# An encoder kernel on one core: in the first layer, the powers of the input matrices are each worked out from the raw matrices, held in PSUM

## The reference, cut to what matters

```
a_bar = exp(lam * dt)                                  # complex, one per state
b_bar = ((a_bar - 1.0) / lam)[..., None] * b_mat       # b_mat = b_re + i b_im
bu    = einsum('gph,bsgh->bsgp', b_bar, u)
states[s] = a_bar * states[s-1] + bu[s]                # in both directions
```

## Time and profile before

| | |
|---|---|
| median of 3 runs | 1513.65 us (1512.05 to 1514.21) |
| the profiled execution | 1514.12 us, of which the traced span is 1512.3 us |
| busy over the span | PE 94%, PEld 77%, DVE 76%, ACT 59%, POOL 22% |
| GpSimd's products (lines 394 to 400) | all in the two mixers |
| mean DMA rate | 248 GB/s |
| mean granted clock of TensorE | 0.979 of full speed |

### The profile page before, as it was taken

How to read it: one execution, slowest core, us unless ns; L and a number is a source line. 1 busy time by engine, 2 the same in 40 slices (tenths; PEclk the granted TensorE clock), 3 DMA queues, 4 the chain that set the end, 5 groups by cost and what they waited for, 6 DMA issues and landing times.

```text
span 1512.3 us, 24141 instructions
## 1 busy us (share of the span) xinstructions
PE 1421.9 (94%) x8701; PEld 1163.8 (77%) x8701; DVE 1145.3 (76%) x1098; ACT 897.7 (59%) x988; POOL 336.2 (22%) x427
## 2 busy tenths in 40 slices
PE   4689999999998999898999999999999999999995
PEld 3567778788887788677888888878888888788884
DVE  6965656755546477576889889988898889888985
ACT  4335454543435365645767776767677767776774
POOL 3895740999100077100000000000000000000000
PEclk9899899999999999998999999999999999999998
DMA  9242144555554433594999999999999999999970
GB/s 262 94 170 72 57 139 168 180 184 183 190 166 167 144 95 113 172 336 141 366 353 338 364 333 347 361 320 362 343 338 362 330 351 365 314 363 331 349 255 28
DMA packets 273809, 374.65 MB, mean 248 GB/s; under 512 B 17616, under 2 KB 220752, under 8 KB 273616
## 3 DMA queue, kind: packets, MB, share of 16 engines
q1 hardware_dynamic: 270176, 367.51, 71.7%
q0 software_dynamic: 1280, 3.15, 1.1%
q10 hardware_dynamic: 2288, 3.11, 0.6%
HBM read 371.63 MB, written 1.05 MB: 246 GB/s over the span
## 4 chain that ended last, share of the span: by engine, by line
PE 79%; DVE 9%; ACT 5%; issue 4%; DMA 1%; SPq 1%; POOL 0%; ACTq 0%; DVEq 0%; POOLq 0%
PE bank L579 76%; ACT hi L1050 3%; DVE lo L1411 3%; SPq L454 1%; PE bank L980 1%; PE bank L597 1%; DVE raw L394 1%; DVE at_lo L1836 1%; DVE raw L396 1%; DMA areg<-in_norm_mix_dram 1%; DMA raw<-in_w_out_dram 1%; DVE at_lo L1806 1%; DVE at_lo L1425 0%; ACT at_hi L1062 0%; PE bank L894 0%
## 5 line engine op out<-in xcount | busy, mean ns | idle before, releaser
L1411 DVE TENSOR_TENSOR lo<-raw,hi 128x2048 fp32r<-128x2048 f32 x347 | 804.0, 2322 | 176.7 <-ACT hi L1050 167.7
L1050 ACT ACTIVATE hi<-raw 128x2048 fp32r<-128x2048 f32 x347 | 662.9, 1914 | 133.8 <-PE bank L579 131.2
L579 PE MATMUL bank<-hi,at_hi 128*128 128x512 f32 x1280 | 519.7, 406 | 37.7 <-DVE lo L1411 12.2
L579 PE MATMUL bank<-hi,at_lo 128*128 128x512 f32 x1280 | 505.2, 395 | 0.0
L579 PE MATMUL bank<-lo,at_hi 128*128 128x512 f32 x1280 | 504.4, 394 | 0.0
L579 PEld LDWEIGHTS bank<-hi,at_hi 128*128 128x128 f32 x1280 | 243.9, 191 | 93.3 <-DVE lo L1411 22.8
L579 PEld LDWEIGHTS bank<-hi,at_lo 128*128 128x128 f32 x1280 | 243.1, 190 | 52.7
L579 PEld LDWEIGHTS bank<-lo,at_hi 128*128 128x128 f32 x1280 | 244.4, 191 | 46.5
L579 PE MATMUL bank<-hi,ht_hi 128*128 128x512 f32 x440 | 172.2, 391 | 4.4 <-DVE ht_lo L1737 3.5
L579 PE MATMUL bank<-lo,ht_hi 128*128 128x512 f32 x440 | 171.3, 389 | 0.0
L579 PE MATMUL bank<-hi,ht_lo 128*128 128x512 f32 x440 | 171.3, 389 | 0.0
(11 more groups left out here) (248 smaller groups left out, 1134.2 us busy)
## 6 DMA issues: line engine op xcount, KB each, us to landing
raw<-in_moe_w_dram SPq DMA_DIRECT2D x528, 512.0 KB, 5.3
raw<-in_ffn_w_dram SPq DMA_DIRECT2D x66, 512.0 KB, 4.2
raw<-in_w_in_dram SPq DMA_DIRECT2D x64, 512.0 KB, 4.6
raw<-in_w_branch_dram SPq DMA_DIRECT2D x16, 512.0 KB, 4.2
raw<-in_w_out_dram SPq DMA_DIRECT2D x16, 512.0 KB, 6.3
raw<-in_w_glu_dram SPq DMA_DIRECT2D x4, 512.0 KB, 4.2
xres<-in_x_dram SPq DMA_DIRECT2D x2, 512.0 KB, 6.4
areg<-in_norm_mix_dram ACTq DMA_DIRECT2D x2, 512.0 KB, 6.5
```

Of the source, the lines that this page charges most:

```text
L579: return pe.matmul(o, a, b, start=start, stop=stop)
L1050: act.activation(hi[:, slot, :], src, ACT.Copy).then_inc(hi_ready, 1)
L1411: tt(lo[:, slot, :], src, hi[:, slot, :].bitcast(f32), SUB).then_inc(lo_ready, 1)
```

## The change

On TensorE, `raw_matrices` comes between tiles t+1 and the `"ct"` transposes: two matmuls by the identity copy the raw input matrices (real part, imaginary part) to the two `PY` banks. On VectorE, `next_factor` first works out the three factors `coef[k]` = coefficient x a_bar^(k+1) on 128x64 arrays, and then each of the four results is made by `input_power` straight from the raw matrices in `PY`: the multiplications by the real part of the factor go to SBUF, those by the imaginary part go to `PV` banks, and the halves are put together with one operand from SBUF and one from PSUM. The multiplications run over the whole bank and only the last step over the two pieces. The wait for `b_part` in `inner` moves ahead of the two matmuls that clear `PY`. Layer 1 and GpSimd's work stay as they are.

```diff
+        coef = area(15616, 192).rearrange("p (k r c) -> p k r c", k=3, r=2)
+        coef_tmp = [area(2048 + 64 * i, 64).rearrange("p (r c) -> p r c", r=2) for i in range(2)]
...
                 if l == 0:
                     pe.wait_ge(loads, 32)
+                pe.wait_ge(b_part, l + 1)
                 for bank in PY:
                     mm(bank[:, 0:448], ident, cst[:, C_TRI:C_TRI + 1].broadcast_to([P, 448]), True, False)
                 pe.wait_ge(kdiag_ready, l + 1)
-                pe.wait_ge(b_part, l + 1)
                 pe.wait_ge(c_ready, l + 1)
...
+            def raw_matrices():
+
+                pe.wait_ge(bc_in, BC_LOADS)
+                for r in range(2):
+                    m = mm(PY[r][:, :], ident, braw[:, r].rearrange("p q d h -> p (q d h)"), True, True)
+                m.then_inc(braw_full, 1)
...
                 proj(t + 1, l, 0, 4, False, True)
                 if l == 0:
+                    raw_matrices()
                     states_numbers_t(0)
...
+            def next_factor(k):
+
+                def times(i):
+                    return par[:, i:i + 1, 0:32].broadcast_to([P, 2, 32])
+                src = par[:, CO_RE:CO_IM + 1, 0:32] if k == 0 else coef[:, k - 1]
+                tt(coef_tmp[0], src, times(A_RE), MUL)
+                own.step(tt(coef_tmp[1], src[:, ::-1, :], times(A_IM), MUL))
+                tt(coef[:, k, 0], coef_tmp[0][:, 0], coef_tmp[1][:, 0], SUB)
+                own.step(tt(coef[:, k, 1], coef_tmp[0][:, 1], coef_tmp[1][:, 1], ADD))
+
+            def input_power(dst, k):
+
+                def factor(r):
+                    f = par[:, CO_RE + r, 0:32] if k == 0 else coef[:, k - 1, r]
+                    return f.rearrange("p (q d) -> p q d", d=2).unsqueeze(3).broadcast_to([P, PAIRS, 2, GC])
+
+                def whole_bank(bank):
+                    return bank[:, :].rearrange("p (q d h) -> p q d h", q=PAIRS, d=2)
+                t1 = bt[0]
+                for r in range(2):
+                    tt(t1[:, r], whole_bank(PY[r]), factor(0), MUL)
+                for r in range(2):
+                    last = tt(whole_bank(PV[r]), whole_bank(PY[1 - r]), factor(1), MUL)
+                own.step(last)
+                for q0, q1, aps in dst:
+                    tt(aps[0], t1[:, 0, q0:q1], whole_bank(PV[0])[:, q0:q1], SUB)
+                    last = tt(aps[1], t1[:, 1, q0:q1], whole_bank(PV[1])[:, q0:q1], ADD)
+                own.step(last)
...
                 if l == 0:
-                    dve.wait_ge(bc_in, BC_LOADS)
-                    product(tt, own, whole(bbar), whole(braw), 0, CO_RE, CO_IM, bt, False)
+                    for k in range(3):
+                        next_factor(k)
+                    dve.wait_ge(braw_full, 1)
+                    input_power(whole(bbar), 0)
                 split_static(t + 3)
...
-                    product(tt, own, b_power(1), whole(bbar), 0, A_RE, A_IM, bt, False)
+                    input_power(b_power(1), 1)
                 split_static(t + 4)
                 if l == 0:
-                    product(tt, own, b_power(2), b_power(1), 0, A_RE, A_IM, bt, False)
+                    input_power(b_power(2), 2)
                 split_static(t + 5)
                 if l == 0:
-                    product(tt, own, b_power(3), b_power(2), 0, A_RE, A_IM, bt, False)
+                    input_power(b_power(3), 3)
                     dve.memset(dve_mark, 0.0).then_inc(b_part, 1)
```

More of the change, by code:

```diff
@@ L213, in build @@
         v_ready = sem("v_ready")
+        braw_full = sem("braw_full")
         b_part, b_ready, c_ready = sem("b_part"), sem("b_ready"), sem("c_ready")
```

## The result

The changed kernel takes 1501.39 us in the median of seven runs (1499.07 to 1508.29), beside 1512.05 us for the kernel before in its seven (1509.36 to 1518.41): a ratio of 0.9935, 95% interval 0.9917 to 0.9953. Forecast were 1502.7 us and a ratio of 0.9927. When the same kernel was run again later it gave 1502.60 beside 1512.46 us, a ratio of 0.9934 (0.9917 to 0.9952). So the change is worth some 10 us.

What follows compares the result with a forecast made beforehand. VectorE, taking turns with GpSimd, was taken to bound the first mixer. Stalls and slow starts of 3.6 + 6.4 + 3.2, less 1.8 for copies and 0.4 at the transposes, gave 11.0 us: 1502.7 us, range 1500.5 to 1506.7.

Steps and rivals of the forecast that it cites:

- Who takes turns: VectorE beside GpSimd: instructions with two SBUF inputs last about 1.35 us each; with one PSUM input about 0.65 for 512 columns.
- Rival B: VectorE's products: the new instructions take turns with GpSimd as well, a power costs 9.1 us, gain 2.4 us; chance 0.05.
- its half for the subtractions: VectorE's products: only the subtractions take turns, a power costs 6.3 us, gain 9.3 us, time 1504.4; chance 0.08.
- 1. The copies: TensorE ahead of the "ct" transposes: two copies take 1.8 us and move t+2 and GpSimd's start 1.8 us later.
- 2. The factors: VectorE before the products: 12 small instructions, 2.4 us (1.8 to 3.4), hidden behind the copies.
- 3 and 4. `bbar`, the powers, the splits: VectorE: `bbar` 3.9 us, each power 4.2 instead of 13.3, each split 2.8, `b_part` at 63.6 instead of 76.7.
- 5. TensorE: Tiles t+2 to t+5: both stalls and slow starts gone, t+5 ends at 67.4 instead of 78.8, 11.4 us gained.
- 6. GpSimd: Before the "b" transposes: 7.1 us of contention goes, `b_ready` between 104.2 and 107.6, taken as 107.0, loss 0.4 us.
- The sum: Whole kernel: 11.4 - 0.4 = 11.0 us gained, carried through to the end, median 1502.7 us; chance 0.62.
- Rival A: GpSimd becomes the bound: `b_ready` comes at 110, the gain is 8.0 us, time 1505.7; chance 0.18.
- Rival C: Wait at the "b" transposes turns TensorE's clock down; over 11 us at half speed makes the kernel slower; chance 0.03.

Runs made afterwards that it cites:

- experiment 5: Changed kernel with ScalarE's gate block g0 ahead of its split of t+8: 1502.67 us; with power 4 moved from GpSimd to VectorE too: 1496.15 us, again 1495.90.

## Why the prediction was right, point by point

**Who takes turns: right.** A power in five arrangements, from the rows above: both inputs in SBUF beside a busy GpSimd 13.3 us (12 instructions) and 11.3 (8), one kind of instruction with a PSUM input 7.7 or 6.6, all of them 3.96, and 4.26 with both in SBUF and GpSimd idle. The rule of the Trainium skill, SBUF — State Buffer, "Who interferes with whom", describes each of these. Rival B, and its half for the subtractions, have fallen (0.55 us at 47.51). The rule of the Trainium skill that spoke against the change, VectorE: DVE Perf Modes, the section on the TRN2 errata, would have had 120 - 58 = 62 cycles more for each, by the prediction's estimate from that page 0.06 us. It does not show here: with a PSUM input two multiplications of 512 columns take 1.27 to 1.29 us (45.00 and 38.18), with two SBUF inputs beside an idle GpSimd 1.29. The prediction compared 0.68 us for one instruction with 1.29 for two; like with like is 1.27 to 1.29 with 1.29, so that a PSUM input neither costs nor saves anything beside an idle GpSimd.

**1. The copies: right.** They take 1.88 us in the row and move the `"ct"` transposes by 1.71 us against a common point ahead of them (the profile of after begins 0.6 us earlier there); forecast were 1.8.

**2. The factors: right.** They take 2.1 us, forecast 2.4, and VectorE waits 1.15 us for the copies all the same (the bracket of its first multiplication): hidden.

```profile
36.85 0.18 DVE L1517 TENSOR_TENSOR raw<-raw 128x32 f32<-128x32 f32 x1
38.18 1.29 DVE L1529 TENSOR_TENSOR raw<-bank,par 128x512 f32<-128x512 f32 x2 [1.15 <-PE bank L582]
...
41.31 0.68 DVE L1535 TENSOR_TENSOR raw<-raw,bank 128x512 f32<-128x512 f32 x1
```

**3 and 4. `bbar`, the powers, the splits: right, a little dear.** A power is 3.96 us for 4.2, a split 2.6 to 3.05 for 2.8. `b_part` is at 61.96, forecast 63.6.

**5. TensorE: right, with a term missed in each direction.** t+4 and t+5 have no wait. Tile t+6 begins at 72.47, forecast 71.5. Tile t+2 began earlier than forecast (42.55 for 43.3), but behind its 1.73 us wait seven matmuls run at half speed (0.76 us, then 0.63 where 0.39 is usual), and t+2, t+3 and the transposes of u take 57.11 - 42.55 = 14.6 us for 13.05: 1.5 us that the sum did not have. Before, the same wait had left the clock up. Part of it comes back behind t+6. That tile begins with 0.47 us now and 0.77 before, but it turns slow at its third matmul and runs some eight at half speed, for twelve before; tiles t+6 and t+7 take 13.4 us for 14.4. The first two rows are after, the third is t+8 of before:

```profile
73.32 0.63 PE L582 MATMUL bank<-hi,at_hi 128*128 128x512 f32 x1
...
85.89 0.47 PE L582 MATMUL bank<-hi,at_hi 128*128 128x512 f32 x1 [0.67 <-DVE areg L1475]
...
97.37 0.47 PE L579 MATMUL bank<-hi,at_hi 128*128 128x512 f32 x1 [0.74 <-DVE areg L1464]
```

Both are within the spread of one slow start more or less, 1.6 us, that the range had.

**6. GpSimd: the sum right, the way there not.** `b_ready` came at 106.86, forecast 107.0, and the wait at the transposes is 1.05 us for 0.4. From GpSimd's start to the mark it is 106.86 - 41.88 = 65.0 us, forecast 64.4, before 68.7. But `c_ready` came at 74.83 and not near 70. I had split the contention by chains as if the splits of VectorE stayed where they were. They moved up with the products: more of them fall into the three powers of the output matrices (c_ready at 74.8 for 67.4), fewer into the phase tables, which took 98.77 - 74.83 = 23.9 us for the 29.5 of before, and none into power 4, which took 8.1 us for 12.7. All nine splits from t+3 to t+11 fall into GpSimd's time, where before eight did: the sum held because it counted them together. `c_ready` isn't wanted before 98 us, so its delay cost nothing.

**The sum: right, with some luck.** 11.0 us were forecast at the `"b"` transposes and 10.96 measured in the profiles, or 10.3 without the 0.6 us that the profile of after was ahead already; at the first turn it is 127.83 - 116.44 = 11.4. The medians have 10.7 and 9.9 us, the ratios 9.8 and 10.0. That it comes so close is partly luck: the clock took 1.5 us at t+2 and gave back 1.0 at t+6 and t+7, and the sum had neither.

**Why the profile shows 15.1.** Between the start of the `"b"` transposes and the ACT table load behind the turns, before takes 219.39 - 117.98 = 101.4 us and after 204.56 - 107.02 = 97.5. The window of the turns of after, and below it that of the changed kernel run again, whose profiled execution took 1508.02 us:

```profile
107.00:205.00 98.00, 90.32 (x1121) 72.18 (x1122) 63.59 (x108) 53.76 (x130) 70.67 (x112) 0.95 0.30 87
```

```profile
107.00:205.00 98.00, 92.14 (x1094) 73.82 (x1095) 57.85 (x96) 49.18 (x124) 70.54 (x111) 0.87 0.25 76
```

The granted clock is 0.95 and 0.87 for the same program, where before has 0.91 over the same stretch. In the second execution the turns end at 211.00, so that the stretch takes 103.9 us and the gain there is 8.4. Of this 2.3 us more are lost further on, about 1 by the second mixer's start and 1.5 in the turns of layer 1, in parts that the change leaves as they are: at the end it is 6.1. Its stretch begins so:

```profile
107.11 3.68 PE L582 MATMUL bank<-cst,raw 64*64 64x64 f32 x64 [2.95 <-POOL small L1956]
...
119.10 0.67 PE L582 MATMUL bank<-qk,ureg 64*128 64x256 f32 x2 [0.75 <-issue]
```

There t+2 had kept its clock, TensorE reached the transposes earlier and waited 2.95 us for 1.05, and the transposes ran at half speed: the first turn begins 2.7 us later though `b_ready` came within 0.1 us. From the first turn on, after takes 88.1 us at a granted clock of 0.94 where this execution takes 91.9 at 0.89 and before 91.6 at 0.91. So 11 us are the change, and the 4 beyond them go with the clock of that one execution. Rival A (the bound at `b_ready`, time lost to it) is half right: GpSimd is the bound now, but at 106.9 and not 110. Rival C is right in its mechanism and wrong in its size here: the late `b_ready` costs clock in the transposes, 1.4 to 2.6 us up to the first turn beyond the delay of `b_ready` in the three profiles with waits of 2.95, 5.78 and 7.49 us, and not the over 11 us that would have made the kernel slower. It foretold slow turns as well, and for these no run shows the wait as their cause: the turns were slow without one and fast behind the longest. The changed kernel's runs spread from 1499 to 1508 us. Which of two equal executions keeps its clock in the turns I have not settled.

## What to carry to other kernels

When VectorE and GpSimd work side by side and VectorE's instructions all last as long as GpSimd's whatever their size, put one input of each VectorE instruction into PSUM before anything else: here a 1.9 us copy on TensorE turned 13.3 us a product into 4.0. Then look at what is wanted from the engine that gained nothing: its slack, 8.5 us here, was spent at once, and the next microseconds were on GpSimd and not on VectorE (both edits of experiment 5 together gave 6.7 us more). And look at the clock behind a wait: here waits of 2.95 to 7.49 us ahead of small matmuls made the first of these slow, which cost 1.4 to 2.6 us beyond the wait. Beyond that don't read the clock off one profile, since two executions of one kernel differed by up to 9 us.

## What the runs showed of the hardware that I had not expected

- The result's place does not matter: with two SBUF inputs and a PSUM output a VectorE multiplication of 512 columns takes 1.6 us beside GpSimd, with one PSUM input 0.64 to an SBUF or a PSUM output alike.
- Fewer and larger instructions help little where two engines take turns: 12 instructions of 384 and 128 columns took 13.3 us, 8 of up to 512 columns 11.3 us, and the kernel was no faster.
- After a wait of 2.95 to 7.49 us the first 64 transposes of 64x64 take 3.50 to 3.68 us, after one of 0.34 or 1.05 us 2.08. After a wait of 1.73 us both occurred at tile t+2: 0.76 us for the first matmul in one execution and 0.47 in another of the same kernel.
